# Two reorderings in TensorE's delta stage, one activation table set, and two transfers moved, in a two-block transformer kernel on one Trainium2 core

## The reference, cut to what matters

```
z = einsum('bhqd,bhkd->bhqk', q, k) * scale
log_1m = where(causal, log_sigmoid(-z), 0)
log_after = cumsum(log_1m, reverse) - log_1m
w = where(causal, exp(log_sigmoid(z) + log_after), 0)
out = einsum('bhqk,bhkd->bhqd', w, v)
```

```
lower = where(strict, (k_beta @ k.T) * decay, 0)
u, w = triangular_solve(lower + eye, [v * beta, k_beta * exp(g)])
v_new = u - w @ state
o = (q * exp(g)) @ state + attn @ v_new
state = state * exp(g_last) + k_dec.T @ v_new
```

## Time and profile before

| | us |
|---|---|
| median of 3 runs (lowest, highest) | 2659.49 (2655.54, 2660.88) |
| profiled execution | 2660.03 |
| its span, first to last instruction | 2658.2 |
| PE busy | 2501.1 (94%) |
| DVE busy | 1840.2 (69%) |
| ACT busy | 1111.9 (42%) |
| table loads of ACT in the attention, lines 702 and 710 | 8 (10.3 us) and 7 (9.0 us) |
| DMA | 407.60 MB, 153 GB/s over the span |

### The profile page before, as it was taken

One profiled execution on the slowest core, in us unless ns is written; L12 is line 12 of the kernel. 1 busy time (PEld: TensorE's weight loads), 2 busy tenths in 40 slices (PEclk: granted clock), 3 DMA queues, 4 the chain that ended last, 5 costly groups with the idle time before them and its releaser, 6 DMA issues.

```text
span 2658.2 us, 37704 instructions
## 1 busy us (share of the span) xinstructions
PE 2501.1 (94%) x15010; PEld 2146.3 (81%) x15010; DVE 1840.2 (69%) x3121; ACT 1111.9 (42%) x1720; POOL 65.0 (2%) x64
## 2 busy tenths in 40 slices
PE   5889999978799889999999899999999999998998
PEld 3848999956699868888886588888888888877997
DVE  2656999854476767777866677676876666876665
ACT  4465446833454542222445452222442222554443
POOL 1000000112000000000000000000000000000000
PEclk8989999989899989999999999999999999998999
DMA  7866996643266536665522035565455454432663
GB/s 251 265 204 199 284 285 186 160 134 119 83 183 186 168 97 172 174 174 162 131 62 76 25 118 164 153 167 155 125 148 152 137 151 126 122 85 72 185 186 106
DMA packets 632564, 407.60 MB, mean 153 GB/s; under 512 B 27751, under 2 KB 588614, under 8 KB 631366
## 3 DMA queue, kind: packets, MB, share of 16 engines
q1 hardware_dynamic: 631712, 404.94, 53.2%
q10 hardware_dynamic: 678, 0.25, 0.0%
HBM read 404.09 MB, written 1.05 MB: 152 GB/s over the span
## 4 chain that ended last, share of the span: by engine, by line
PE 85%; DVE 6%; ACT 4%; DMA 2%; issue 1%; SPq 1%; ACTq 0%; POOL 0%; DVEq 0%; POOLq 0%
PE ps L1739 72%; PE ps L1761 2%; PE ps L578 1%; PE ps L1776 1%; PE ps L841 1%; PE ps L855 1%; DMA raw<-in_attn_w_in 1%; PE ps L1530 1%; ACT w_hi L1933 1%; DVE w_lo L2097 1%; PE ps L1503 1%; DVE rstd L1579 1%; DVE p L1589 1%; PE ps L1517 0%; DVE ada_acc L2114 0%
## 5 line engine op out<-in xcount | busy, mean ns | idle before, releaser
L1933 ACT CAST w_hi<-raw 128x1024 fp32r<-128x1024 f32 (+3 forms) x557 | 555.3, 997 | 1196.6 <-PE ps L1739 1165.0
L1739 PE MATMUL ps<-h_hi,w_hi 128*128 128x258 f32 (+2 forms) x2952 | 975.6, 330 | 25.0 <-DVE h_lo L2311 13.8
L1739 PE MATMUL ps<-h_lo,w_hi 128*128 128x258 f32 (+2 forms) x2952 | 965.1, 327 | 0.0
L1739 PE MATMUL ps<-h_hi,w_lo 128*128 128x258 f32 (+2 forms) x2952 | 964.1, 327 | 0.0
L2097 DVE TENSOR_TENSOR w_lo<-raw,w_hi 128x1024 fp32r<-128x1024 f32 (+3 forms) x557 | 644.7, 1159 | 263.1 <-ACT w_hi L1933 260.3
L1739 PEld LDWEIGHTS ps<-h_hi,w_hi 128*128 128x128 f32 x2952 | 561.7, 190 | 83.7 <-issue 25.4
L1739 PEld LDWEIGHTS ps<-h_hi,w_lo 128*128 128x128 f32 x2952 | 561.6, 190 | 47.8 <-issue 2.2
L1739 PEld LDWEIGHTS ps<-h_lo,w_hi 128*128 128x128 f32 x2952 | 561.2, 190 | 46.8
L1739 PE MATMUL ps<-a_hi,w_hi 128*128 128x256 f32 (+1 forms) x1056 | 354.6, 336 | 0.5 <-DVE a_lo L2152 0.5
L1739 PE MATMUL ps<-a_lo,w_hi 128*128 128x256 f32 (+1 forms) x1056 | 353.2, 334 | 0.0
L1739 PE MATMUL ps<-a_hi,w_lo 128*128 128x256 f32 (+1 forms) x1056 | 353.2, 334 | 0.0
(11 more groups left out here) (351 smaller groups left out, 2290.4 us busy)
## 6 DMA issues: line engine op xcount, KB each, us to landing
raw<-in_ffn_w_in SPq DMA_DIRECT2D x264, 512.0 KB, 4.7
ada_raw<-in_w_mod SPq DMA_DIRECT2D x120, 512.0 KB, 3.9
raw<-in_ffn_w_out SPq DMA_DIRECT2D x96, 512.0 KB, 5.2
ada_raw<-in_ada_w SPq DMA_DIRECT2D x40, 512.0 KB, 5.5
wide_rows<-in_ada_w SPq DMA_DIRECT2D x40, 512.0 KB, 4.9
raw<-in_ffn_w_out SPq DMA_DIRECT2D x48, 384.0 KB, 3.7
raw<-in_gdn_w_in SPq DMA_DIRECT2D x33, 512.0 KB, 4.1
raw<-in_w_in SPq DMA_DIRECT2D x26, 512.0 KB, 3.9
```

What stands on the lines that cost most here:

```text
L1739: last = mm(ps[0:m, slot, 0:n], w[:, slot, k * P:k * P + m], v[:, s0 + k, c0:c0 + n], start=(k == 0 and w is w_hi and v is hi), stop=(k == ...
L1933: nc.scalar.copy(w_hi[:, slot, 0:n], raw[:, slot, 0:n]).then_inc(s_hi, 1)
```

## The change

Five lines on ACT, PE and SP. At the start of the attention ACT asks for one named table set, `natural_log_exp_and_others`. In a delta level, `wide_products` moves from the end of the level to between the first and second products; where a level has none, the next pair's products move there instead; the step of the pair before moves from ahead of the second products to behind them. A level that has both keeps the next pair's products at the end. SP issues the first two wide loads (4 transfers) ahead of the next stage's 4 weight tiles. The lists of DVE, POOL and, apart from the table set, ACT stay as they were.

```diff
+LN_EXP = "natural_log_exp_and_others"
...
         def attention_scalar(act, st):
+            act.preload_act_table_set(LN_EXP)
             for m in range(4):
...
                     merge(gr, level)
                     if level > 1:
                         turn_inverse(gr, level)
-                    if gr:
-                        steps[level](gr - 1)
-                    if level:
-                        merge2(gr, level)
-                    if gr < 3 and level in ahead:
-                        ahead[level](gr + 1)
                     if (gr, level) in WIDE_STEPS:
                         i = WIDE_STEPS.index((gr, level))
                         wide_products(pe, 2 + i // KD, i % KD)
+                    elif gr < 3 and level in ahead:
+                        ahead[level](gr + 1)
+                    if level:
+                        merge2(gr, level)
+                    if gr:
+                        steps[level](gr - 1)
+                    if (gr, level) in WIDE_STEPS and gr < 3 and level in ahead:
+                        ahead[level](gr + 1)
                     if (gr, level) in ((1, 4), (3, 5)):
                         wide_turned(pe, 2 + gr // 2)
...
                 elif st[0] in ("attention", "delta"):
+                    wides = [(n, k) for n, w in enumerate(WIDES) if w[1] == st[0] for k in range(KD)]
+                    for n, k in wides[:2]:
+                        wide_load(sp, n, k)
                     for j in range(RING):
                         load(stages[i + 1], j)
                         ahead.add(stages[i + 1].g0 + j)
-                    for n, w in enumerate(WIDES):
-                        if w[1] == st[0]:
-                            for k in range(KD):
-                                wide_load(sp, n, k)
+                    for n, k in wides[2:]:
+                        wide_load(sp, n, k)
```

## The result

| | us |
|---|---|
| kernel before, median of 20 runs (lowest, highest) | 2657.1 (2650.98, 2660.88) |
| changed kernel, median of 20 runs (lowest, highest) | 2660.95 (2656.27, 2666.14) |
| ratio, 95% interval | 1.0016 [1.0009, 1.0023] |
| profiled execution, its span | 2659.12, 2657.3 |

The change makes the kernel slower by 0.16%, 4.3 us (2.4 to 6.1). The forecast was 0.18% and 4.9 us. The single profiled execution is 0.9 us shorter than that of before, of which 1.8 us lie ahead of the attention, where the code is the same. The 20 executions of either kernel lie 10 us apart, so what follows is read stage by stage.

What follows compares the result with a forecast made beforehand. PE was taken as the bound, 85% of the chain. Attention -5.0, delta's order +8.9, clock +1.0 and SP's order 0 gave +4.9 on 2660.03, so 2664.9 (2664.4 for a median); 8 in 10 within 2655 to 2670.

Steps and rivals of the forecast that it cites:

- Attention, -5.0: Stick-breaking half: 15 table loads go, two PE waits shrink, fewer clock falls, 1.13 us waits stay; -5.0 us (-3.4 to -5.9).
- Levels without steps, -2.0: Delta, pair 0: levels 2, 3 and 6 gain from blocks between the products, level 1 loses 0.5; -2.0 us in sum.
- Levels with steps: Delta, pairs 1 to 3: DVE takes the step's result before the subtraction PE waits for; +10.9 us.
- Clock, +1.0: Delta, level 3 of pairs 1 and 3: about 1.9 us idle may drop PE's clock; +1.0 us (0 to +4).
- SP's order, 0: Four transfers ahead of the next stage's tiles: nothing gained, delay hidden, up to +2 if transfers slow; taken as 0.
- falls at every level 3: Rival: clock falls more often, at each pair's level 3 and the attention's end; +4 us, 2668.5; chance 0.18.
- The table set was kept: Answers the rival that the set isn't kept and the loads stay: no attention gain, 2670; chance 0.05.
- the DMA wait and the clock give it back: Rival at 168.38: modulation rows land in time and no clock falls in delta and at 207; 2659.5; chance 0.22.
- Steps cost nothing: Rival in delta: DVE's copies finish under the second products, delta about -1, table gain -6 and more; 2651.5; chance 0.10.

Runs made afterwards that it cites:

- e1: The kernel before with only the named table set added on ACT; 2651.44 us, ratio 0.9977.
- e9: The kernel before with the table set and SP's new order, PE's delta order as before; 2650.02 us, ratio 0.9976.
- e4: The changed kernel, with DVE taking a step's result behind the subtraction instead of ahead of it at levels 1 to 4; 2648.53 us, ratio 0.9963.
- e3: The kernel before with only SP's new order of transfers; 2657.85 us, ratio 1.0.

## Why the prediction was right

Its sum was +4.9, and the runs give +4.3 (2.4 to 6.1). Its mechanism held in both stages. The sum is somewhat closer than its parts, and that is luck: the sticks gained 1.4 us more than forecast, and the levels lost 0.5 more. Within the levels, too, errors cancel: pair 3 lost 1.4 us less than forecast, the clock cost 1.0 more.

- *Attention, -5.0.* 16 loads went, not 15; since only PE's waits were priced, that changes nothing in the sum. The waits fell as worked out: 2.19 to 1.28 (forecast 1.27), 3.75 to 1.98 (forecast 2.05), and the 1.13 stayed. The sticks are 6.4 us shorter in the changed kernel and 5.0 in e1; the difference is the clock behind the last wait, of which half a fall was counted. It fell in e1 (0.8 us saved there) and not in the changed kernel (2.1 saved), so -6.4 lies past the bound of -5.9: a fall spared at the end was worth more than the 1.6 taken. The softmax stretch, 2.1 us shorter in the changed kernel, is no part of this (e9).
- *Levels without steps, -2.0.* Measured -1.8 in pair 0; 4.52 for 5.36 where 4.43 was forecast, since the second products came at 2.49, not 2.4.
- *Levels with steps.* Second to next first products: 2.80 (forecast 2.79), 3.48 to 3.52 at level 3 (3.48), 2.31 at level 5 (2.31). Pair 1 +5.2, of which 2.0 are a clock fall, so +3.2 for a forecast of +3.5; pair 2 +2.3 for +1.8. In pair 3 +3.3 for +4.7: level 1 was costed at half clock, and there PE was at full clock, 4.88 instead of 6.35. The tail grew by 0.8 (0.95). Level 0, costed at nothing, took 0.6 more in sum.
- *Clock, +1.0.* One fall, at 596.60, cost 2.0: (1, 4) took 6.62 for 5.30 in pair 2, (1, 5) 5.39 for 4.69.
- *SP's order, 0.* 1.0 [0.9991, 1.0009]. The added wait of the first tile is there and hidden.
- Levels in sum: 140.6 - 130.2 = +10.4 for +9.9 with the clock.

Of the rivals, falls at every level 3 were not met: one came, in pair 1. The table set was kept. The one by which the DMA wait and the clock give it back named the right place and wasn't met: the wait stayed at 1.36 and the product behind it at half speed. "Steps cost nothing" is refuted by the changed kernel and became true in e4, when DVE's list was changed.

## What to carry to other kernels

Moving work into another engine's idle time is half of an edit: look in the list of the engine that consumes it, and ask whether its wait now stands ahead of something ready that the critical engine needs (here 10.9 us lost, and 12.4 won back by two lines on DVE). When 20 us of table loads bring 6, find the in-order operation behind which they were hidden, and remove both (14.6 us). The three parts of this change, of both signs, add up, so time such parts one by one before judging the sum.

## What the runs showed of the hardware

- An idle time of 1.91 us ahead of the first products was followed by a fall of the clock behind 596.60 (the second products then took 2.05 for 1.13), and by none at 667.64, in the same execution. The kernel with PE's order alone lost the clock at the same level, (1, 4), and not in pair 3, so the place repeated in the two profiles that have this order; what tells the places apart isn't known. The Trainium skill, "TensorE: Matmul & The Clock Gate", section "HAM oscillation — how this bites in real kernels", has PE throttled again by DMA waits between bursts of matmuls, waits that are longer in its example than the 1.91 us here. The fall at (1, 4) is no case of that, so here the trace goes beyond the page. After 1.98 us at the end of the attention the clock fell in e1 and stayed in the changed kernel and in e9.
- The stretch behind delta, the same code in all, took between 1946.0 and 1950.8 us. 4.8 us, 0.18%, is as much as the whole effect, and one profile alone couldn't have shown it. Between the kernel before (1950.5) and e3 (1946.0) it is PE's clock: PE is busy for 1889.5 and 1884.7 us there with the same work, and in the last 450 us the granted clock is 0.96 and 0.97.
